# First mixer of a two-layer trunk: the queries' unit ahead of the gate unit, the gate unit in four column strips, modulation sums ahead of a filter combination

## What is computed

```python
mc = adaln(c_pre, w_mod[i], b_mod[i])           # silu(c) @ w_mod + b_mod, in six parts
hs = modulate(xs, ms[0], ms[1])                 # rms_norm(x) * (1 + scale) + shift
...
q_a, k_a, v_a, r_a, z_f, z_b, q_g, k_g, v_g = jnp.split(h @ w_in, EVEN_SPLITS, axis=-1)
log_f = (jax.nn.log_sigmoid((z_f @ w_gf + b_gf).astype(jnp.float32)) / GLA_TAU).reshape(B, L, H_A, DK_A)
log_b = (jax.nn.log_sigmoid((z_b @ w_gb + b_gb).astype(jnp.float32)) / GLA_TAU).reshape(B, L, H_A, DK_A)
...
filt = implicit_filters(L, wf1, bf1, freq, wf2, bf2, wf3)   # of the second layer, long convolution
```

## Time and profile before

| | us |
|---|---|
| median of 3 runs | 1649.03 |
| lowest, highest | 1647.98, 1649.09 |
| the profiled execution | 1648.96 |
| its span in the trace | 1646.9 |
| TensorE busy | 1604.1 (97%) |
| VectorE busy | 1080.4 (66%) |
| ScalarE busy | 734.9 (45%) |
| GpSimd busy | 37.1 (2%) |

### The profile page before, as it was taken

How to read it: one execution, slowest core, us unless ns; L and a number is a source line. 1 busy time by engine, 2 the same in 40 slices (tenths; PEclk the granted TensorE clock), 3 DMA queues, 4 the chain that set the end, 5 groups by cost and what they waited for, 6 DMA issues and landing times.

```text
span 1646.9 us, 27708 instructions
## 1 busy us (share of the span) xinstructions
PE 1604.1 (97%) x11345; PEld 1475.7 (90%) x11345; DVE 1080.4 (66%) x1873; ACT 734.9 (45%) x1303; POOL 37.1 (2%) x42
## 2 busy tenths in 40 slices
PE   6999999999999999999998999999999999999997
PEld 3589888799989999999998996678999999999997
DVE  5634662768857847846874367744888488587585
ACT  5434462646624424523544434343665154254254
POOL 0000000001000000000002002000100000000000
PEclk9999999999999999999999999999999999999999
DMA  9456532136345544545234112001632223233222
GB/s 318 145 181 201 176 129 66 51 78 132 116 143 157 151 126 131 153 129 154 71 110 147 54 44 86 26 1 51 124 88 84 71 78 96 60 99 85 74 65 90
DMA packets 239143, 178.49 MB, mean 108 GB/s; under 512 B 8309, under 2 KB 232651, under 8 KB 238380
## 3 DMA queue, kind: packets, MB, share of 16 engines
q1 hardware_dynamic: 236084, 171.48, 34.5%
q0 software_dynamic: 2016, 4.59, 2.0%
q10 hardware_dynamic: 920, 0.69, 0.2%
HBM read 163.67 MB, written 8.49 MB: 105 GB/s over the span
## 4 chain that ended last, share of the span: by engine, by line
PE 88%; DVE 5%; ACT 3%; SPq 2%; issue 1%; DMA 1%; ACTq 0%; DVEq 0%
PE ub L1107 7%; PE ub L1109 7%; PE ub L1108 7%; PE ua L1107 6%; PE ua L1109 6%; PE ua L1108 6%; PE ua L1529 6%; PE ua L1531 5%; PE ua L1530 5%; PE ub L1529 5%; PE ub L1531 5%; PE ub L1530 5%; PE pm L1023 2%; PE ua L1374 2%; PE ub L1374 1%
## 5 line engine op out<-in xcount | busy, mean ns | idle before, releaser
L2119 ACT ACTIVATE whi<-weight_sums 128x1024 fp32r<-128x1024 f32 x88 | 93.2, 1059 | 71.8 <-DVE weight_sums L2804 47.3
L1529 PE MATMUL ua<-x_mixed_high,whi 128*128 128x322 f32 x352 | 110.6, 314 | 1.9 <-ACT snap L2193 1.8
L1529 PE MATMUL ub<-x_mixed_high,whi 128*128 128x322 f32 x352 | 111.0, 315 | 0.7 <-ACT snap L2193 0.7
L1531 PE MATMUL ua<-x_mixed_high,wlo 128*128 128x322 f32 x352 | 109.2, 310 | 0.0
L1531 PE MATMUL ub<-x_mixed_high,wlo 128*128 128x322 f32 x352 | 109.2, 310 | 0.0
L1530 PE MATMUL ub<-x_mixed_rest,whi 128*128 128x322 f32 x352 | 109.0, 310 | 0.0
L1530 PE MATMUL ua<-x_mixed_rest,whi 128*128 128x322 f32 x352 | 109.0, 310 | 0.0
L1107 PE MATMUL ub<-hidden_high,whi 128*128 128x384 f32 (+1 forms) x324 | 102.2, 316 | 6.5 <-DVE x L2872 3.5
L2777 DVE TENSOR_TENSOR wlo<-weight_sums,whi 128x1024 fp32r<-128x1024 f32 x88 | 107.2, 1218 | 1.5 <-ACT whi L2119 1.4
L1107 PE MATMUL ua<-hidden_high,whi 128*128 128x384 f32 (+1 forms) x324 | 101.1, 312 | 1.8 <-DVE x L2872 1.8
L1109 PE MATMUL ub<-hidden_high,wlo 128*128 128x384 f32 (+1 forms) x324 | 100.4, 310 | 0.0
(11 more groups left out here) (663 smaller groups left out, 4984.0 us busy)
## 6 DMA issues: line engine op xcount, KB each, us to landing
raw<-in_w_ffn_in SPq DMA_DIRECT2D x88, 512.0 KB, 5.5
mod_late<-in_w_mod SPq DMA_DIRECT2D x24, 1024.0 KB, 5.4
raw<-in_w_ffn_out SPq DMA_DIRECT2D x48, 384.0 KB, 4.3
modw<-in_w_mod SPq DMA_DIRECT2D x16, 1024.0 KB, 5.2
raw<-in_w_in_even SPq DMA_DIRECT2D x10, 1024.0 KB, 9.2
raw<-in_w_in_odd SPq DMA_DIRECT2D x7, 1024.0 KB, 5.9
mod_first<-in_w_mod SPq DMA_DIRECT2D x5, 1024.0 KB, 11.9
ssq<-sq POOLq DMA_DIRECT2D x14, 320.0 KB, 4.6
```

The costliest lines, as they stand in the source:

```text
L1529: pe.matmul(dst, wh[:, c], xh, start=first, stop=False, skip_group_check=True)
L1531: ins = pe.matmul(dst, wl[:, c], xh, start=False, stop=last, skip_group_check=True)
L2119: act.activation(ring(whi, g, w), src, ACT.Copy).then_inc(g_hi, 1)
```

## The change

- The queries' unit becomes unit 0 and the gate unit becomes unit 1. `EVEN_COLS` and the unit names are exchanged.
- The gate unit loads 32 columns instead of 128. ScalarE copies them whole to `zw` and no rest part is made. `gate_unit` multiplies them in full fp32 with the high and the rest part of the input, eight row blocks in four column strips of the array: 32 matmuls, 16 of 384 and 16 of 256 tokens. Each strip j holds the sum over two row blocks, in partitions 32j to 32j + 31; `zz` has 128 rows now, and the gate matrices stand four times in `wgate`, so that the gate products add the four strips.
- The four gate products move into unit 2 (keys), at its sixteenths 3, 5, 9 and 11, with two pairs of banks in turn.
- The modulation pieces 8 and 9 stand together right behind the gate unit; the others stand one unit earlier each, and the last unit has none. SP's queue is reordered for that, and the load of the next units' weights goes ahead of the spectra's store.
- On VectorE `mod_reduce(0)` and what follows it, with the first two `h_scaled`, goes ahead of the fourth `filter_combine`. The tiles `ffb` and `hdif` have other places.

```diff
-MOD_AT = 3
+MOD_AT = 2
...
+        zw = sb("gate_rank_weights", [P, 32 * KD], at=sb_at["whi1"])
...
-        zz = ta("zz", [32, T])
+        zz = ta("zz", [P, T])
...
-        wgate = sb("wgate", [32, 2, 256], at=sb_at["vg"] + 3072)
+        wgate = sb("wgate", [P, 2, 256], at=sb_at["vg"] + 3072)
...
-            return (m, m + 1) if n >= MOD_AT else ()
+            return (m, m + 1) if n >= MOD_AT and m < NMOD else ()
...
-            return raw[1] if n in (21, 23) else modw[mod_slot(n)[0]]
+            return raw[1] if n == 22 else modw[mod_slot(n)[0]]
...
-        EVEN_COLS = [(1536, 128), (0, 256), (256, 256), (512, 256), (768, 256), (1024, 256),
+        EVEN_COLS = [(0, 256), (1536, 32), (256, 256), (512, 256), (768, 256), (1024, 256),
...
-        Z_U, QA_U, KA_U, VA_U, QG_U, KG_U, VG_U = 0, 1, 2, 3, 6, 8, 10
+        QA_U, Z_U, KA_U, VA_U, QG_U, KG_U, VG_U = 0, 1, 2, 3, 6, 8, 10
...
-            sp.dma_start(wgate[0:16, 0, :], i_["w_gla_gate_f"][0]).then_inc(s_const, 16)
-            sp.dma_start(wgate[16:32, 1, :], i_["w_gla_gate_b"][0]).then_inc(s_const, 16)
+            for j in range(0, P, 32):
+                sp.dma_start(wgate[j:j + 16, 0, :], i_["w_gla_gate_f"][0]).then_inc(s_rows, 16)
+                sp.dma_start(wgate[j + 16:j + 32, 1, :], i_["w_gla_gate_b"][0]).then_inc(s_rows, 16)
...
             even_load(0)
             even_load(1)
+            mod_load(8, 8)
+            mod_load(9, 8)
+            even_load(2)
             sp.wait_ge(g_ev, 10)
             sp.dma_start(spilled, gspec[:, :, :]).then_inc(g_out, 16)
-            even_load(2)
+            even_load(3)
...
-            for n in range(MOD_AT, 7):
-                even_load(n)
-                for m in mods_in(n):
-                    mod_load(m)
+            mod_load(10)
+            mod_load(11)
+            even_load(4)
...
                 ins.then_inc(unit_done, 1)

+            def gate_unit(u):
+
+                pe.wait_ge(w_lo, u + 1)
+                for kk in range(2):
+                    for x_ in (hhi, hlo):
+                        for half, t in ((0, slice(0, T1)), (1, slice(T1, T))):
+                            for j in range(4):
+                                k = 4 * kk + j
+                                ins = pe.matmul(ub[32 * j:32 * j + 32, half, 0:(T1, T2)[half]], zw[:, 32 * k:32 * k + 32],
+                                                x_[:, k, t].bitcast(F32), start=kk == 0 and x_ is hhi,
+                                                stop=kk == 1 and x_ is hlo)
...
+
             def gate_mult(n):

                 d, g = n // 2, n % 2
-                if n >= 1:
-                    pe.wait_ge(gate_x, n)
-                else:
+                if n >= 2:
+                    pe.wait_ge(gate_x, n - 1)
+                elif n == 0:
                     pe.wait_ge(vec_c, 2)
-                    pe.wait_ge(unit_free[0], 1)
-                    pe.wait_ge(rs_ready, 1)
-                pe.matmul(pm[:, 0:T1], wgate[:, d, g * P:(g + 1) * P], zz[:, 0:T1], start=True, stop=True)
-                pe.matmul(pt[:, 0:T2], wgate[:, d, g * P:(g + 1) * P], zz[:, T1:T], start=True, stop=True
+                    pe.wait_ge(unit_free[1], 1)
+                left, right = (ub[:, 0], ub[:, 1]) if n % 2 == 0 else (ub[:, 2], pt)
+                pe.matmul(left[:, 0:T1], wgate[:, d, g * P:(g + 1) * P], zz[:, 0:T1], start=True, stop=True)
+                pe.matmul(right[:, 0:T2], wgate[:, d, g * P:(g + 1) * P], zz[:, T1:T], start=True, stop=True
                           ).then_inc(gate_mm, 1)
...
             def head_slots(n):
                 k = n - QG_U - 1
                 at = {a: (lambda p=p: level_pass(p, n)) for a, p in LEVEL_SLOTS.get(n, {}).items()}
+                if n == KA_U:
+                    at = {a: (lambda i=i: gate_mult(i)) for i, a in enumerate((3, 5, 9, 11))}
...
             for n, (c0, w) in enumerate(EVEN_COLS):
                 mods = mods_in(n)
-                beside = {1: 0, 2: 2}
+                inside = mods if n > MOD_AT else ()

                 def middle():
-                    if n in beside:
-                        gate_mult(beside[n])
-                    else:
-                        mod_mm(mods[1], mod_buffer(mods[1]))
-                if n in (2, 3):
-                    gate_mult(2 * n - 3)
+                    mod_mm(mods[1], mod_buffer(mods[1]))
                 if n < 2:
                     pe.wait_ge(g_ev, (5, 8)[n])
+                if n == Z_U:
+                    gate_unit(n)
+                    continue
                 if mods:
+                    mod_mm(mods[0], mod_buffer(mods[0]))
                     if n == MOD_AT:
-                        pe.wait_ge(gate_x, 4)
-                    mod_mm(mods[0], mod_buffer(mods[0]))
+                        mod_mm(mods[1], mod_buffer(mods[1]))
                 for s_, v_ in BEFORE.get(n, ()):
                     pe.wait_ge(s_, v_)
                 unit(n, n % 2, KD, w, hhi, hlo, ready=(h_lo, 0) if n == 0 else None,
-                     turned=n in (VA_U, VA_U + 1, VG_U), middle=middle if mods or n in beside else None,
+                     turned=n in (VA_U, VA_U + 1, VG_U), middle=middle if inside else None,
                      slots=head_slots(n))
                 if n == 0:
-                    pe.wait_ge(s_rows, 16 * 11)
+                    pe.wait_ge(s_rows, 16 * (11 + 8))
                     pe.wait_ge(g_ev, 10)
                     pe.transpose(pt[:, 0:P], vrow[:, :], ident[:, :]).then_inc(vec_t, 1)
-                if n == 6:
+                if n == 5:
                     mod_tr(1)
...
-                act.activation(whi[s][:, 0:width], raw[s][:, 0:width], ACT.Copy).then_inc(w_hi, 1)
+                dst = zw[:, :] if u == Z_U else whi[s][:, 0:width]
+                act.activation(dst, raw[s][:, 0:width], ACT.Copy).then_inc(w_hi, 1)
...
             mod_row(0)
-            filter_combine(3)
             mod_reduce(0)
...
             for k in range(KD):
                 h_scaled(k)
-                if k == 3:
+                if k == 1:
+                    filter_combine(3)
+                elif k == 3:
                     filter_combine(4)
...
-                dve.tensor_scalar(dst[:, 0:T1], pm[:, 0:T1], b, None, ALU.add)
-                dve.tensor_scalar(dst[:, T1:T], pt[:, 0:T2], b, None, ALU.add).then_inc(gate_x, 1)
+                left, right = (ub[:, 0], ub[:, 1]) if n % 2 == 0 else (ub[:, 2], pt)
+                dve.tensor_scalar(dst[:, 0:T1], left[:, 0:T1], b, None, ALU.add)
+                dve.tensor_scalar(dst[:, T1:T], right[:, 0:T2], b, None, ALU.add).then_inc(gate_x, 1)
...
             for n in range(N_EVEN_U - 1):
-                mods = mods_in(n)
-                if n in (2, 3):
-                    gate_copy(2 * n - 3)
-                if n == 7:
+                if n == 6:
                     mod_reduce(1)
-                w_rest(n + 1, (n + 1) % 2, KD * EVEN_COLS[n + 1][1])
+                if n + 1 == Z_U:
+                    dve.wait_ge(w_hi, n + 2)
+                    dve.sem_inc(w_lo, 1)
+                else:
+                    w_rest(n + 1, (n + 1) % 2, KD * EVEN_COLS[n + 1][1])
...
-                if n in (1, 2):
-                    gate_copy(2 * n - 2)
-                if n == MOD_AT:
+                if n == KA_U:
+                    for g in range(4):
+                        gate_copy(g)
+                elif n == VA_U:
                     decays()
-                elif n == MOD_AT + 1:
+                elif n == VA_U + 1:
                     first_queries()
```

47 lines of the change are left out of this document (27 added, 20 removed).

## The result

The changed kernel takes 1640.54 us, the median of five executions (1638.79 to 1644.12), beside 1649.03 us of the kernel before (1647.98 to 1651.39, five executions): ratio 0.9942, 95% interval 0.9925 to 0.9959, or 8.5 us less where 6.1 us were forecast. The direction was right, and so were most of the terms; one term, the four gate products, was put at nothing and was not, so the size was missed. Two later sets of executions of both kernels gave 0.9953 (0.9932 to 0.9973) and 0.9941 (0.9923 to 0.9960).

The account below looks back on a forecast made before the run. TensorE, busy 97% of the span, was taken as the bound. Terms 7.5 - 4.6 + 0.6 + 1.1 + 1.5 made 6.1 us less than 1649.03, so 1642.9 us, range 1641.2 to 1646.5.

Parts of the forecast that it names:

- Gate unit: On TensorE, the old unit's 7.5 us goes; the new one, four column strips abreast, takes 4.6 us (4.3 to 5.0).
- The gate products: Four products moved into the keys' unit, claimed to cost TensorE the same from 128 rows as from 32; no gain.
- Wait of 0.6 us: TensorE's wait before the second unit, for VectorE's rest part of the weights, goes: 0.6 us saved.
- Wait of 1.1 us: TensorE's wait before the first piece of modulation weights, for VectorE's last gate copy, goes: 1.1 us saved.
- Slow stretch: Partly half clock at 110 to 114 us, after the 1.1 us wait, goes with it: 1.5 us saved, 1.7 at most.
- Start-up: Before the first unit: weights land later, fourth filter combination starts at 50.7 us, last row block 72.1; TensorE cost 0.
- Keys' unit: Third unit: its weights are ready at 86.0 us, TensorE is busy until 87.3; covered with 1.3 us to spare.
- rival D: The queries' copy waits for the spectra's slow store, so the keys' weights come late: slower, 1651.3 us; 4%.
- A: In gate unit and modulation pair, narrow strips let the clock fall: gain 4.4 or 2.7 us, 1644.6 to 1646.3; 10%.
- E: In the gate unit, strips don't run abreast, so it takes 17.2 us: 1655.5 us; 2%.
- B: At start-up, first weights land 1 to 3 us late and the first unit waits for row blocks: 1644 to 1646; 12%.
- C: The slow stretch at 110 us isn't caused by idle time, or moves elsewhere: 1.5 us less gain, 1644.4; 8%.

## Why the prediction was wrong in size

By its steps:

- **Gate unit.** 4.6 us forecast with 4.3 as the lower end, 4.34 measured. I stood "nearer the lower end", for a changing-over cost once. Measured with the 0.18 us by which the first strip matmul starts later behind the transposition than a full one, it is 4.5 us, so that cost was about right. The four strips go abreast almost perfectly: 17.2 us by the earlier trace rows over 4.34 is 3.96 times, over 4.52 it is 3.8. The Trainium skill's ratio of 2.38 for three strips (page "TensorE: Matmul & The Clock Gate", Measured speedup vs the span model) would have made it 5.4 us by my estimate; the trace does not agree with it here.
- **The gate products, the step that failed.** "The products themselves cost the same, they have only 128 instead of 32 rows." They fell from 1.27 to 0.89 us each, 1.5 us in all, three fifths of what was missed. The hint was in the trace: the earlier trace rows shows the product's start at 81.38, and the unit goes on at 82.65, 1.27 us later, where 640 columns at 0.86 us for 512 are 1.07. A product from 128 rows does cost its columns, 1.07 us in full; I had never asked what the old one cost, 1.46 us, 0.39 of it for standing with 32 rows among full ones. The two runs that change only the rows settle the cause.
- **Wait of 0.6 us.** Gone as forecast. But one profile was taken as the rule; over six it is 1.1 us, 0.5 more. I named it a wait for VectorE and did not draw the conclusion that its length is whatever TensorE's start leaves, and so differs between executions.
- **Wait of 1.1 us.** Gone, and 1.0 us of work (0.4) was measured for it alone.
- **Slow stretch.** 1.6 us in the two profiled executions, as forecast; on average 1.0 us. The step holds with the condition that it is a matter of chance for each execution.
- **Start-up.** Forecast 50.7 us for the fourth combination, 50.64 measured; last row block at 72.1, measured 71.07 + 1.01 = 72.08; spill issued at 71.5, measured 71.55. In this profile unit 0 was not held up. It began 0.5 us later because TensorE waited longer for the first modulation weights (2.11 instead of 1.22 us ahead of 30 us), which the change doesn't touch. In the other two profiles of the changed kernel it was held up, by 0.8 us each: the sign that I had named for the forecast being wrong ("if the first unit waits for row blocks"). "Cost taken: 0" was the right price only for a start-up that the slow clock delays, as in the profile that I forecast from.
- **Keys' unit.** Ready 86.0 forecast, 84.25 + 2.29 = 86.54 measured, TensorE there at 87.24: covered, by 0.7 us and not by 1.3. ScalarE's copy of the queries began at 81.12, right behind the unit's end, so the spill had landed and rival D did not occur.
- **Modulation pair.** "Cost 0": 1.84 us together instead of 2.00. That fits a cost of going to 32 column strips and back that is paid once, which no run separates. Against it, the keys' tiles took 0.5 us more. That is mostly no cost of its own: each product costs 1.07 us in full and 0.89 start to start, and the 0.18 us left stand four times in this unit, 0.7 us, where about 0.2 us stood before.

Summed as an average execution has it: 3.2 + 1.1 + 1.5 + 1.1 + 0.2 - 0.5 = 6.6 us of work, with 7.0 us (0.3) measured, and 1.0 us for the clock at 110 us with 1.6 (0.8) measured. Against the 4.6 us of work in the forecast (7.5 - 4.6 + 0.6 + 1.1), 2.4 us of work were missed: 1.5 for the products, 0.5 for the wait of 0.6 us, 0.3 for the gate unit. The 1.5 us forecast for the clock agree with the 1.6 measured only within that error, and part of the agreement is luck, since the stretch at 110 us gives 1.0. The named terms at their best make 7.5 - 4.3 + 0.6 + 1.1 + 1.7 = 6.6 us, 1642.4; the low end of 1641.2 left 1.2 us beyond them, and a term set to zero with no bounds was larger than that. Of the rivals, A (the strips let the clock fall) and E did not occur. B's wait came in two of three profiles, but not by B's cause: there the fourth combination began without a wait for ScalarE, so the first weights were not late; what was late was VectorE's own chain. C is wrong in its cause, but its price is right in two of five profiles of the kernel before, which have no slow stretch to lose.

## What to carry to other kernels

A matmul that uses 32 of 128 rows among full ones costs more than its columns say, so pad it to full rows with zeros if the operands allow (here 0.38 us for each of four in the rows; the time of that edit alone did not show it). An edit that is "the same but larger" needs a bound like any other term. When an idle time is removed from TensorE, look at the clock behind it, and at several profiles of it: what follows an idle time of 1 us is a matter of chance, and so is a wait for another engine whose length depends on when TensorE arrives.

## What the hardware showed that was not expected

- Row count matters: a product of 640 columns among full matmuls takes 1.27 us start to start from 32 rows and 0.89 us from 128 (1.46 and 1.07 us in full), in both kernels. The Trainium skill's page "TensorE: Matmul & The Clock Gate" (Why this matters for your kernels) says that a single matmul from 32 rows takes the same time as one from 128. Among full matmuls the rows here say otherwise.
- Four column strips of fp32 matmuls ran 3.8 to 3.96 times as fast as single ones, 4.3 us in a row with the clock at 2.4 GHz.
- Waits of 1.10 and 1.45 us were followed by a stretch at 1.2 GHz in three of five and in six of seven profiles. The mean granted clock of single executions goes from 0.985 to 0.998, and the spread of the times goes with it: the work of the kernel before scatters by 1.5 us from one execution to the next (the standard deviation), its span by 2.9 us.
- Slow stretches of 17 us from about 30 us on were seen in three profiles, all of kernels with the changed start-up (two of the changed kernel), and in none of six with the old one. Whether the transfers that it adds bring them was not tried.
